# Down projection of a two-layer decoder trunk: six of each eight output tiles by seven block products instead of eight, with the residual parked in device memory

## The reference

```python
def swiglu(x, wg, wu, wd):
    return (jax.nn.silu(x @ wg) * (x @ wu)) @ wd
...
            x = x + 0.5 * swiglu(rms_norm(x, n_ffn1[i]), w_ffn1_gate[i], w_ffn1_up[i], w_ffn1_down[i])
            mix, v, new_buf, hT = hybrid_mix(
...
            x = x + mix
            x = x + 0.5 * swiglu(rms_norm(x, n_ffn2[i]), w_ffn2_gate[i], w_ffn2_up[i], w_ffn2_down[i])
            gate = jax.nn.sigmoid(rms_norm(x, n_ple[i]) @ w_ple_gate[i])
            x = x + gate * (p @ w_ple_proj[i])
```

## Time and profile before

| | |
|---|---|
| median of 3 runs | 1888.15 us (1887.84 to 1888.51) |
| the profiled execution's own time | 1887.87 us |
| its span, first to last instruction | 1885.7 us |
| PE busy | 1850.9 us, 98% |
| DVE busy | 1371.3 us, 73% |
| ACT busy | 946.9 us, 50% |
| POOL busy | 215.7 us, 11% |
| DMA traffic | 233.42 MB, mean 124 GB/s |

### The profile page before, as it was taken

One profiled execution on the slowest core, in us unless ns is written; L12 is line 12 of the kernel. 1 busy time (PEld: TensorE's weight loads), 2 busy tenths in 40 slices (PEclk: granted clock), 3 DMA queues, 4 the chain that ended last, 5 costly groups with the idle time before them and its releaser, 6 DMA issues.

```text
span 1885.7 us, 37225 instructions
## 1 busy us (share of the span) xinstructions
PE 1850.9 (98%) x15112; PEld 1831.2 (97%) x15112; DVE 1371.3 (73%) x2041; ACT 946.9 (50%) x1363; POOL 215.7 (11%) x261
## 2 busy tenths in 40 slices
PE   6999999999999999999999999999999999999996
PEld 6999999998999999999999999999999999999996
DVE  7867848768688577587687587577785875866775
ACT  6635526446456255365465264454544653634553
POOL 0000000340110000002110000013202000000012
PEclk9999999999999999999999999999999999999998
DMA  5635546522345464454345364463222545635541
GB/s 159 157 108 147 144 106 155 161 79 68 91 104 153 113 151 129 118 151 144 101 105 145 101 163 128 125 169 112 68 90 90 135 124 131 151 115 134 144 136 46
DMA packets 65724, 233.42 MB, mean 124 GB/s; under 512 B 7376, under 2 KB 9712, under 8 KB 65568
## 3 DMA queue, kind: packets, MB, share of 16 engines
q1 hardware_dynamic: 52576, 184.87, 30.6%
q0 software_dynamic: 12992, 46.32, 14.8%
HBM read 228.86 MB, written 2.31 MB: 123 GB/s over the span
## 4 chain that ended last, share of the span: by engine, by line
PE 96%; DVE 2%; ACT 1%; DMA 1%; issue 0%; DVEq 0%; SPq 0%; ACTq 0%
PE main L773 21%; PE main L633 20%; PE main L599 18%; PE main L638 10%; PE aux L633 8%; PE aux L773 6%; PE aux L638 4%; PE aux L863 2%; PE main L678 2%; PE aux L599 1%; PE aux L811 1%; PE main L863 1%; PE aux L883 0%; DVE rstd_b L1356 0%; DMA w_lo<-weights_dram 0%
## 5 line engine op out<-in xcount | busy, mean ns | idle before, releaser
L959 ACT ACTIVATE w_hi<-raw 128x1024 fp32r<-128x1024 f32 (+1 forms) x184 | 187.4, 1030 | 118.5 <-PE main L773 66.0
L633 PE MATMUL main<-part_hi,w_hi 128*128 128x260 f32 x960 | 240.8, 283 | 3.7 <-DVE tmp L1495 3.7
L633 PE MATMUL main<-part_lo,w_hi 128*128 128x260 f32 x960 | 240.8, 283 | 0.0
L1344 DVE TENSOR_TENSOR w_lo<-raw,w_hi 128x1024 fp32r<-128x1024 f32 (+1 forms) x184 | 221.9, 1207 | 23.2 <-ACT w_hi L959 22.1
L773 PE MATMUL main<-part_hi,w_lo 128*128 128x260 f32 x1080 | 217.5, 283 | 0.0
L773 PE MATMUL main<-part_hi,w_hi 128*128 128x260 f32 x1080 | 217.1, 282 | 0.0
L773 PE MATMUL main<-part_lo,w_hi 128*128 128x260 f32 x1080 | 216.9, 282 | 0.0
L553 POOL DMA_DIRECT2D w_lo<-weights_dram x80 | 68.8, 860 | 1126.5 <-ACT w_lo L989 1126.5
L599 PE MATMUL main<-part_hi,w_hi 128*128 128x260 f32 x944 | 192.6, 285 | 2.0 <-DVE tmp L1489 2.0
L599 PE MATMUL main<-part_hi,w_lo 128*128 128x260 f32 x944 | 189.8, 283 | 0.0
L599 PE MATMUL main<-part_lo,w_hi 128*128 128x260 f32 x944 | 189.4, 282 | 0.0
(11 more groups left out here) (250 smaller groups left out, 3982.0 us busy)
## 6 DMA issues: line engine op xcount, KB each, us to landing
raw<-weights_dram SPq DMA_DIRECT2D x344, 512.0 KB, 3.7
w_lo<-weights_dram POOLq DMA_DIRECT2D x80, 512.0 KB, 6.5
x<-x_in_dram SPq DMA_DIRECT2D x4, 520.0 KB, 6.9
y_out<-x SPq DMA_DIRECT2D x8, 260.0 KB, 2.6
mix<-p_in_dram POOLq DMA_DIRECT2D x2, 520.0 KB, 4.0
tau<-ln_dram POOLq DMA_DIRECT2D x2, 512.0 KB, 3.8
tau<-ws_dram POOLq DMA_DIRECT2D x2, 512.0 KB, 6.1
bs<-bs_dram POOLq DMA_DIRECT2D x2, 256.0 KB, 4.0
```

The lines of the kernel that those rows point to most:

```text
L633: pe.matmul(ps, hi_w[:, w], xx(k), start=(start and k == 0 and b == 0), stop=False, skip_group_check=True)
L959: act.activation(w_hi[:, s, 0:c], raw[:, s, 0:c], ACT.Copy).then_inc(whi, 1)
L1344: dve.tensor_tensor(w_lo[:, s, 0:c], raw[:, s, 0:c], w_hi[:, s, 0:c], ALU.subtract).then_inc(wlo, 1)
```

## The change

In the two chunks of 8 hidden tiles, six of the eight down units go in three pairs through the same seven-product scheme; the pair of output tiles 0 and 1 stays direct. A pair is again a 2x2 by 2x2 block product: two output tiles, the chunk's eight hidden tiles taken as four even and four odd ones, two token halves. The third chunk's down units stay direct.

The three pairs of a chunk stand at the head of the next chunk's sequence of tiles (`down_pairs`, `tiles_of`), so the sequences are now 6, 3+8 and 3+6 tiles, 26 for a network instead of 20.

What comes with it:

- **Sums of hidden blocks.** DVE makes four sums from each pair of hidden tiles (`sums_raw`: three instructions on 520, 260 and 260 elements), ACT cuts their high part (`sums_hi`, 1040 elements) and DVE the low part (`sums_lo`, 1040 elements), four times in each of the two chunks. The sums live in `x` (raw), `xs` (low, the same bytes as `x`), and free halves of other buffers.
- **The residual leaves SBUF.** `x` is written to device memory (`x_spill`) before each network but the first. At the end of the network it is loaded again.
- **Down results go to device memory.** Each output tile of the first two chunks is scaled on DVE and sent with a DMA to `d_part` (64 DMAs of 128x520). Two DMAs with an addition bring them back onto `x`: `d_part[0]` and `d_part[1]`, 128x4160 each.
- All these DMAs are issued by POOL, in one sequence with `gate_low`. DVE waits in `free` until a result buffer has been sent, and for `reload_s` before the third chunk's results are added to `x`.
- `softplus` (25 tiny DVE instructions, once) moves from a direct down unit into tile steps of the second chunk, in three parts.

```diff
+DOWN_PAIRS = KH - 1
+DOWN_CHUNKS = sum(t == XT for t in FFN_CHUNKS)
+TILES = HT0 - LEAD + DOWN_CHUNKS * DOWN_PAIRS
...
             def gates(l, which):
 
-                for t in range(S_TILES):
-                    gate_low(l, which, t)
...
+                    for t in range(tiles_of(c)):
+                        gate_low(n + 2 * t, S + t)
+                        if c == 0 and t == 1:
+                            copy_lead(f, G)
+                        if c and t == 1:
+                            for j in range(2):
+                                pool.wait_ge(evac, G - 1 + j)
+                                send(c - 1, j, 2 + j)
+                        if c and DOWN_PAIRS <= t < 2 * DOWN_PAIRS:
+                            second_out(t - DOWN_PAIRS)
+                        if c and 2 <= t < 2 + DOWN_PAIRS:
+                            first_out(t - 2)
+                        if c == DOWN_CHUNKS and t == 5:
+                            pool.wait_ge(unit, n + 2 * DOWN_PAIRS)
+                            pool.dma_start(x[:, :, :], x_spill if f else x_in).then_inc(reload_s, 16)
+                        if c == DOWN_CHUNKS and t == 6:
+                            for b in range(4):
+                                pool.wait_ge(d_out[b], 16 * sent_by(f, b))
+                            pool.wait_ge(reload_s, 48 * f + 16)
+                            pool.dma_start(x[:, :, :], d_part[0], accum_op=ALU.add,
+                                           max_dma_last_dim=8 * TOK).then_inc(reload_s, 16)
+                        if c == DOWN_CHUNKS and t == 7:
+                            pool.wait_ge(reload_s, 48 * f + 32)
+                            pool.dma_start(x[:, :, :], d_part[1], accum_op=ALU.add,
+                                           max_dma_last_dim=8 * TOK).then_inc(reload_s, 16)
...
                     def P1(t):
...
-                        product(X(G, t), *gate_w(t, 0), *a11, True, False,
-                                (gate_lo[gate_slot(t)], 16 * ((S + t) // 2 + 1))).then_inc(prod, 1)
+                        product(X(G, S + t), *gate_w(S + t, 0), *(h11 if down(t) else a11), True, False,
+                                (gate_lo[gate_slot(S + t)], 16 * ((S + t) // 2 + 1))).then_inc(prod, 1)
...
+            def sums_raw(f, c, i):
...
+                dve.tensor_tensor(to[:, 0:2, :], v[:, 0:4:3, :] if c == 0 else v[:, 1:3, :],
+                                  v[:, a + 1:a + 2, :].broadcast_to([P, 2, HALF]), ALU.subtract).then_inc(sh_raw, 1)
+                dve.wait_ge(sh_raw, at + 1)
+                dve.scalar_tensor_tensor(to[:, 2, :], v[:, a, :], -1.0, to[:, SUM_AT[c][1], :],
+                                         ALU.mult, ALU.subtract).then_inc(sh_raw, 1)
+                dve.wait_ge(sh_raw, at + 2)
+                dve.scalar_tensor_tensor(to[:, 3, :], v[:, b, :], -1.0, to[:, 2, :],
+                                         ALU.mult, ALU.subtract).then_inc(sh_raw, 1)
...
                     def c12(t):
                         dve.wait_ge(unit, n + 2 * t + 2)
-                        dve.tensor_tensor(T(2 + t % 2)[:, A1], Z(G, t), u2(t), ALU.add).then_inc(evac, 2)
+                        dve.tensor_tensor(second(t)[:, A1], Z(G, S + t), u2(S + t), ALU.add).then_inc(evac, 2)
...
                     def hidden(t):
                         dve.wait_ge(evac, G + 2 * t + 2)
...
+                        if t < pairs:
+                            dve.scalar_tensor_tensor(second(t), second(t), -0.5, rstd_b[:, :],
+                                                     ALU.mult, ALU.mult).then_inc(d_second, 1)
+                            to_send(2 + (S + t) % 2)
...
+                    def tile_sums(t):
                         k = whole - tiles + t
-                        dve.tensor_tensor(lo_[:, k, :], T(2 + t % 2), hi_[:, k, :], ALU.subtract).then_inc(hlo, 1)
+                        if not last and t >= pairs and k % 2:
+                            dve.wait_ge(hf_s, products_of(l, h) + t - pairs + 1)
+                            sums_raw(f, c, k // 2)
+                        if first and t == 2:
+                            sums_raw(f, c, 0)
```

More of the change, by code:

```diff
@@ L267, in trunk @@
         prod = sem("prod")
+        sh_raw = sem("sh_raw")
+        sh_hi = sem("sh_hi")
+        sh_lo = sem("sh_lo")
+        lead_copy = sem("lead_copy")
+        d_second = sem("d_second")
+        d_out = [sem(f"d_out{b}") for b in range(4)]
+        spilled = sem("spilled")
+        reload_s = sem("reload_s")
+        bd_zero = sem("bd_zero")
         p1_copy = sem("p1_copy")
@@ L391, in raw_up, with X, Y, Z @@
             return raw[:, (n + 1) % SLOTS, half * HB:(half + 1) * HB]
[L393 to L404, removed]
+        def X(G, T_):
+            return main[(main_slot(G) + T_) % 2][:, 0, 0:HALF]
+        def Y(G, T_):
+            return main[(main_slot(G) + T_) % 2][:, 1, 0:HALF]
+        def Z(G, T_):
+            return aux[0][:, (main_slot(G) + T_) % 2, 0:HALF]
+        def down_bank(G, which, c, j):
+            if c < DOWN_CHUNKS:
+                return main[(main_slot(G) + first_of[c + 1] - 1) % 2] if j else aux[1]
+            if j == 0 or (j == XT - 1 and not which):
                 return aux[1]
             return main[(main_slot(G) + j + 1) % 2]
+        first_of = [sum(tiles_of(b) for b in range(c)) for c in range(len(FFN_CHUNKS))]
         def xparts(l):
@@ L545, in conv_states, with gate_low @@
                                      xr[:, m % 2, SEQ + 3:SEQ + 3 + NSAMP]).then_inc(pst, 1)
[L547 to L551, removed]
+            def gate_low(n, T_):
                 pool.wait_ge(gate_neg, T_ + 1)
-                pool.dma_start(w_lo[:, gate_slot(t), :], weights[n, :, :],
-                               accum_op=ALU.add).then_inc(gate_lo[gate_slot(t)], 16)
@@ new lines, in tile_sums_lo, with down_out @@
+                    def tile_sums_lo(t):
+                        k = whole - tiles + t
+                        if not last and t >= pairs and k % 2:
+                            sums_lo(l, f, c, k // 2)
+                        if first and t == 2:
+                            sums_lo(l, f, c, 0)
+                    def down_out(j):
+                        dve.wait_ge(unit, d + j + 1)
+                        free(2 + j)
+                        dve.scalar_tensor_tensor(halves(T(2 + j)), pair(down_bank(G, which, c, j)), 0.5,
+                                                 halves(rstd_b[:, :]), ALU.mult, ALU.mult).then_inc(evac, 1)
+                        to_send(2 + j)
@@ L1638, in ffn @@
                             tau_sums(g + 2, (tau1, tau2))
-                        else:
+                        elif last:
                             lo(d, 0)
+                        tile_sums_lo(g - 1)
+                        if f == 0 and c == 1 and g in (2, 3):
+                            softplus(g - 1)
                     t = tiles - 1
```

539 lines of the change are left out of this document (364 added, 175 removed).

## The result

The changed kernel takes 1915.43 us (median of 4 runs, 1914.51 to 1918.64); the kernel before, run beside it, 1888.33 (4 runs, 1887.84 to 1888.66). The ratio is 1.0147, interval 1.0129 to 1.0164: 1.5% slower.

A forecast was written before the change was run, and what follows sets the result against it. PE was taken as the bound, busy 1850.9 of 1885.7 us. 1887.9 - 34.4 (matmuls) + 9.6 (DVE sums) + 1.4 (`softplus`) + 64.4 (queue) + 14 (clock) = 1943 us, 2.9% slower; 8-in-10 range 1890 to 1978.

The forecast's parts named there:

- The matmuls: Paired down units of the first two chunks: 288 fewer matmuls at 0.1193 us each on PE's path, -34.4 us.
- DVE: Steps with hidden sums in each network's first chunk: `c22` comes late and PE waits 2.4 us per network, +9.6 us.
- a sign of a wrong step: If PE waits behind `c22` outside the first chunk, the reckoning of the hidden sums on VectorE is wrong.
- softplus: Its 24 dependent instructions, moved into two tile steps of the first network, exceed the idle time before `c22`: +1.4 us.
- Rival 2: VectorE becomes the bound: all steps with sums last 11.5 us instead of 10.07, 46 us in all, total 1901; chance 0.05.
- The mechanism on the queue: POOL's queue works in order, so `gate_low` stands behind big transfers: PE waits 16.1 us in each network, +64 us.
- the sends and the load: On POOL's queue: the 64 result transfers cost nothing; loading `x` (5.1 us of DMA engines) delays `gate_low(6)` hardly at all.
- One sign: Two PE waits of 5 us or more before a low-third matmul in the last steps of each network.
- Rival 1: The queue holds nothing up to speak of: adding transfers run at 418 GB/s or `gate_low` overtakes; 1864 to 1873, chance 0.17.
- queue plus clock: PE's waits for `gate_low` behind big transfers, 64 us, and slower matmuls after eight long stalls, 14 us.
- The rate of the adding DMA: Transfers adding `d_part` onto `x`: taken as 176 GB/s, 12.1 us of all DMA engines for each 2.13 MB.
- The clock: Behind each of eight long PE stalls the granted clock falls, losing 1.8 us each: +14 us.

## Why the prediction was right in its sign and too high

**The matmuls.** -34.4 said, -33.9 measured by themselves. Right.

**DVE.** +9.6 said, 4 x 1.85 = 7.4 read from PE's timeline, in the two places named. The one wait for `c22` outside the first chunk, which was named as a sign of a wrong step, belongs to `softplus`. Making one set of sums earlier took 3.9 of it back. Rival 2, DVE as the bound of every step with sums, falls: its 46 us are nowhere in PE's waits. `softplus` cost that one wait, 0.64 us from start to start, so about 0.5 us and not 1.4.

**The mechanism on the queue** was right at each step: it works in order, each adding DMA holds up the `gate_low` behind it, two long waits follow in each network, and the sends and the load cost next to nothing (at most some 2 us in all). One sign fails: both waits were to be of 5 us or more, and the second is 1.5, 4.2, 2.3 and 2.5 us in the four networks, for the two reasons given below. The run without the adding DMAs takes away nearly all of the cost, the move behind `gate_low(8)` just the second wait, and the halves make the cost vanish with the same bytes. Rival 1 (the queue holds nothing up to speak of) gave about the right time for a kernel with plain transfers, 1874.81 for its 1864 to 1873, and not for this one.

**What was mis-sized** is the term "queue plus clock": 64 + 14 = 78 us said, 51.4 measured. Two parts of it can be told apart.

- *The rate of the adding DMA.* I took 176 GB/s from two windows of 2 us, each within one `gate_low`, and held against rival 1 that they lie in its middle, so that its start is not in them. Part of it is. In both windows the DMA engines work on POOL's queue (q0) alone, but for one packet of instructions, so nothing else is mixed in. Windows of 1 us show how long a packet takes (packets, MB, share of the 16 engines). In the kernel before, at 204:205, 205:206 and 205.5:206.5:

```profile
q0 software_dynamic: 25, 0.10, 82.3%
q0 software_dynamic: 43, 0.18, 104.6%
q0 software_dynamic: 44, 0.18, 92.9%
```

  And in the second adding DMA of the changed kernel, at 320:321:

```profile
q0 software_dynamic: 52, 0.22, 108.5%
```

  The share times 16 us, divided by the packets, gives 0.53, 0.39 and 0.34 us for one packet of `gate_low`, and 0.33 for one of the big DMA. So the small DMA begins slowly and ends at the pace of the big one. It has 128 packets to bear its start, the big one 512. From 176 to 214 GB/s is a factor of 1.22: 1.10 from the packet's time (0.37 us in the mean of the window at 214.5), 1.09 from the fuller share, 1.02 from rows of 4160 bytes instead of 4096. With 214 GB/s an adding DMA of 2.13 MB is 10.0 us of the engines instead of 12.1, and each of the three `gate_low` 2.5 instead of 3.0: 5.7 us less in each network, 23 in all. In the first network the time from the start of step 3 to the use of `gate_low(8)` came to 52.1 us (281.50, where PE starts it, to 333.55). I had said 57.4; with 214 GB/s the same sum gives 51.7.
- *The clock, counted twice.* I added 1.8 us for each of eight falls on top of the lateness of `gate_low(8)`. But the landing of `gate_low(8)` is set by the queue alone. The slow matmuls between the two waits only make PE arrive later at a wait that ends at a fixed time, so the second wait shrinks by what they lost. In the first network PE would have wanted `gate_low(8)` at 319.37 - 6.82 + 0.12 + 10.07 = 322.7 without either; it came at 333.55, 10.8 late. The waits of 6.82 and 1.74 us from start to start make up 8.3 of it, the slow clock the rest. Only a fall behind the last wait of a network adds to the time, and in this network there was none: the wait of 1.46 us left the clock at full speed, where the other seven long ones halved it.

Taken together, the corrected sum is 51.7 - 41.3 = 10.4 us late in each network, and 1.8 for the clock in three of them: 4 x 10.4 + 3 x 1.8 = 47 us, against 51.4 measured. The rest sits in the later networks. Reckoned as above, `gate_low(8)` is used 10.8 us late in the first network and 12.5, 12.6 and 11.1 in the others, 5.4 us more in all than 4 x 10.4; why the queue is slower there by up to two us was not tried. The whole sum with measured terms is 1887.9 - 33.9 + 7.4 + 0.5 + 51.4 = 1913.3, against 1915.4; some 2 us stay unassigned.

The Trainium skill, "DMA: Bandwidth & Descriptors", section "Anatomy of one DMA — SWDGE (gpsimd) path", was weighed with its 2.0 us plus bytes at 436 GB/s, by which the kernel would have come to near 1873. The adding DMA does not follow it (6.9 us by the rule, 9.95 for the bytes alone at 214 GB/s, 13.9 to 18.8 from issue to landing in the first network). The kernel with plain transfers did come to 1874.81, though its transfers too took 11.5 us beside the other traffic, not 6.9. What the prediction set beside the rule, 3.7 us for `raw`, does not test it, for `raw` goes over SP's queue; the plain DMAs on POOL's queue do, and those of the next line (1.06 MB, 4.4 us by the rule) agree:

```profile
x_spill<-x POOLq DMA_DIRECT2D x6, 1040.0 KB, 4.7
```

The trace decides here as it did in the prediction; only the price was lower than I took it.

What would have helped to choose better: the rows of before had a second reading. A window of 2 us in a DMA whose data moves for some 4 us gives the mean of a slow start and of what follows, and windows of 1 us in the same trace tell the two apart. A packet's time near the end of the small DMA, 0.34 us, was the better price for the long one: 512 x 0.34 / 16 = 10.9 us of all engines instead of 12.1.

## What to carry to other kernels

A big transfer must not stand in a queue ahead of a small one that an engine wants soon. What mattered here was neither the bytes nor how full the DMA engines were, but what stood ahead of the DMA with the least slack: the same additions cost 51 us as two DMAs of 2.13 MB in each network, and nothing that could be measured as four of half the size, two of them behind the last `gate_low`. Before you count a second stall, ask whether it ends at a time that the first one sets or at a time of its own; in the second case what is lost between the two is already in it. And before a load is moved to a free queue, look at what it stands behind in the old one: that order may be what protects a small transfer.

## What the runs showed that I had not expected

- An adding DMA from device memory moves 214 GB/s with the DMA engines full, about half of the 418 of plain loads. In the `gate_low` read above a packet took 0.53 us near the start and 0.34 near the end. Beside other traffic 2.13 MB take 16.7 us in the median against 11.5 for the same transfer without the addition.
- In the changed kernel the seven waits for `gate_low` with 2.3 to 7.8 us of idle time were followed by half the clock, and the one of 1.46 us was not: 0.50 to 0.53 over 5 us behind the longest, 0.66 behind those of 2.3 and 2.5 us. (The ninth, near 46 us, lies between two other waits and tells nothing.) With the load on ACT's queue the wait of 1.84 us was followed by 0.66 too, those of 1.26, 1.28 and 1.71 us by the full clock. The level was as low with the DMA engines idle (share 0.01) as with them full.
- A `gate_low` issued 1.7 us behind a load of 2.13 MB on another queue moved its first bytes only about 4 us after its issue, some 2 us later than usual, in long rows and short ones alike. Why is open: the length of the rows is ruled out as the main cause, and no run here separates what else could hold it back.
